# First two experts of a mixture-of-experts stage written out as straight code without scatter, weight turn and additions; counts loaded inside the first gather

## The reference

```
logits = h2 @ w_router + b_router;  top 4 of 32 experts per token, softmax over the four
for each expert e, over the tokens that chose it:
    hu   = xe @ w_up[e] + b_up[e]            # 1024 -> 2048
    gate = min(hu[:, :1024], 7);  lin = clip(hu[:, 1024:], -7, 7)
    y    = ((lin + 1) * gate * sigmoid(1.702 * gate)) @ w_down[e] + b_down[e]
    out[token] += weight(token, e) * y
x = x + gt_f * out;  y_out = rms_norm(x, g_final)
```

## Time and profile before

| | us |
|---|---|
| median of 3 runs | 1329.02 (1322.39 to 1330.13) |
| span of the profiled execution | 1322.8 |
| TensorE busy | 1189.2 (90%) |
| VectorE / ScalarE / GpSimd busy | 387.1 / 176.3 / 71.6 |
| data moved | 467.22 MB, mean 353 GB/s |

### The profile page before, as it was taken

One profiled execution on the slowest core, in us unless ns is written; L12 is line 12 of the kernel. 1 busy time (PEld: TensorE's weight loads), 2 busy tenths in 40 slices (PEclk: granted clock), 3 DMA queues, 4 the chain that ended last, 5 costly groups with the idle time before them and its releaser, 6 DMA issues.

```text
span 1322.8 us, 23572 instructions
## 1 busy us (share of the span) xinstructions
PE 1189.2 (90%) x8761; PEld 556.1 (42%) x8764; DVE 387.1 (29%) x857; ACT 176.3 (13%) x334; POOL 71.6 (5%) x180
## 2 busy tenths in 40 slices
PE   5999999898989999998999988999877989988996
PEld 4655447645534344443334432444222334333332
DVE  0173215737331221231222121132211221222225
ACT  3002231012101001010111100011110000110101
POOL 1010001323000000000000000000000000000001
PEclk9999999988989999998999998999988999989998
DMA  9934634784569999999999999999999999999992
GB/s 371 358 129 177 225 128 192 223 322 145 235 238 404 396 415 410 422 421 423 421 422 422 422 422 422 422 387 423 423 422 422 422 421 423 420 422 422 423 421 89
DMA packets 80911, 467.22 MB, mean 353 GB/s; under 512 B 8714, under 2 KB 26958, under 8 KB 28778
## 3 DMA queue, kind: packets, MB, share of 16 engines
q1 hardware_dynamic: 78202, 461.75, 85.8%
q10 hardware_dynamic: 2288, 4.37, 1.1%
q0 software_dynamic: 384, 0.59, 0.2%
HBM read 459.66 MB, written 6.42 MB: 352 GB/s over the span
## 4 chain that ended last, share of the span: by engine, by line
PE 65%; DMA 20%; SPq 8%; DVE 3%; issue 3%; POOL 0%; ACT 0%; POOLq 0%; DVEq 0%
PE psum L998 18%; DMA mem<-in_w_up 18%; PE psum L1036 12%; PE psum L1046 8%; SPq L417 7%; PE psum L650 6%; PE psum L965 4%; PE psum L631 3%; PE psum L837 2%; DMA mem<-in_mod_chunks 2%; PE psum L654 2%; PE psum L506 1%; PE psum L758 1%; PE psum L1054 1%; PE psum L1002 1%
## 5 line engine op out<-in xcount | busy, mean ns | idle before, releaser
L998 PE MATMUL psum<-mem 128*32 128x512 f32 (+2 forms) x2432 | 404.3, 626 | 83.8 <-DMA mem<-in_w_up 61.4
L998 PEld LDWEIGHTS psum<-mem 128*32 128x32 f32 (+2 forms) x2432 | 122.2, 122 | 357.5 <-issue 215.8
L1036 PE MATMUL psum<-mem 128*32 128x512 f32 (+3 forms) x1024 | 213.0, 598 | 0.0
L2066 DVE TENSOR_SCALAR mem<-psum 128x256 f32<-128x256 f32 (+3 forms) x32 | 19.2, 601 | 554.8 <-PE psum L1002 554.8
L1046 PE MATMUL psum<-mem 128*128 128x512 f32 (+1 forms) x384 | 152.2, 607 | 2.0 <-issue 1.5
L2087 DVE TENSOR_TENSOR mem<-mem,psum 128x1024 f32<-128x1024 f32 (+1 forms) x96 | 100.3, 1045 | 97.7 <-PE psum L1046 97.7
L1036 PEld LDWEIGHTS psum<-mem 128*32 128x32 f32 (+3 forms) x1024 | 79.6, 128 | 106.2 <-issue 100.0
L965 PEld LDWEIGHTS psum<-mem 128*128 128x128 bf16 x2304 | 77.5, 99 | 20.4 <-issue 20.1
L650 PE MATMUL psum<-mem 128*128 128x512 f32 x192 | 84.2, 595 | 0.0
L965 PE MATMUL psum<-mem 128*128 128x64 bf16 (+1 forms) x2304 | 81.3, 197 | 0.0
L1392 ACT ACTIVATE mem<-mem 128x256 f32<-128x256 f32 (+3 forms) x32 | 17.9, 559 | 465.7 <-DVE mem L2066 465.7
(11 more groups left out here) (275 smaller groups left out, 820.0 us busy)
## 6 DMA issues: line engine op xcount, KB each, us to landing
mem<-in_w_up SPq DMA_DIRECT2D x256, 1024.0 KB, 22.9
mem<-in_w_down SPq DMA_DIRECT2D x128, 1024.0 KB, 17.9
mem<-in_mod_chunks SPq DMA_DIRECT2D x12, 2048.0 KB, 12.2
mem<-in_in_chunks SPq DMA_DIRECT2D x8, 2048.0 KB, 9.8
mem<-in_out_chunks SPq DMA_DIRECT2D x2, 2048.0 KB, 10.0
mem<-in_x_prompt ACTq DMA_DIRECT2D x2, 1024.0 KB, 6.4
mem<-in_state_ret SPq DMA_DIRECT2D x4, 512.0 KB, 8.6
mem<-in_state_mlstm_c SPq DMA_DIRECT2D x4, 512.0 KB, 7.8
```

The source lines that it names most:

```text
L998: last = pe.matmul(out, xg[:, c, cols], moving, start=(c == 0), stop=False)
L1036: last[c] = pe.matmul(psum[slots * q:slots * q + slots, 6 + u, :], turned, piece_slot(home + c, 2, D)[:, piece % 2, 512 * u:512 * u + 512] ...
```

## The change

- The passes of experts 0 and 1 on TensorE are straight code (`expert_without_scatter`): no scatter, no waits on `added` and `y_copied`; pass 0 also has no turn of weights. Pass 1 turns the weights of expert 0 and runs `down(0)`. The loop starts at `FIRST = 2`, and the semaphore counts are shifted accordingly.
- VectorE does no `add_scattered` in passes 0 and 1; ScalarE copies no `G` in pass 0; GpSimd does not clear `G` and `yd`.
- TensorE loads the three first counts before `part2` of the first gather, not after the gather. VectorE computes the counts ahead of the last three `leave_rest` steps.

```diff
@@ gather_first
                 for part in range(3):
+                    if part == 2:
+                        pe.wait_ge(S("counts_ready"), 1)
+                        counted = [count_at(i) for i in range(1, 4)]
                     for t in range(NT):
...
+                return counted
@@ expert (TensorE)
-                gather(ig + 1, count_next, it + 1)
-
-                pe.wait_ge(S("G_ready"), it + 1)
-                pe.wait_ge(S("y_copied"), it + 1)
+                gather(ig + 1, count_next, it)
+
+                pe.wait_ge(S("G_ready"), it - 1)
+                pe.wait_ge(S("y_copied"), it - 1)
...
-                pe.wait_ge(S("added"), 3 * it + 1 + CLEARED)
+                pe.wait_ge(S("added"), 3 * (it - FIRST) + 1 + CLEARED)
...
+            def expert_without_scatter(it, count, count_before, count_next):
+
+                by_size(pe, count, lambda slots: up(it, it, slots))
+                gather(it + 1, count_next, it)
+                pe.wait_ge(S("xg_ready"), it + 2)
+                by_size(pe, count, lambda slots: turn_activations(it, slots))
+                pe.wait_ge(S("gate_ready"), it + 1)
+                pe.wait_ge(S("lin_clipped"), it + 1)
+                if it == 0:
+                    return
+                turn_weights(it, 2)
+                by_size(pe, count_before, lambda slots: down(it - 1, slots, False))
+                pe.wait_ge(S("G_ready"), it)
...
-            gather_first()
-            pe.wait_ge(S("counts_ready"), 1)
...
-            with pe.Fori(0, NE) as e:
+            first, second, third = gather_first()
+            expert_without_scatter(0, first, None, second)
+            expert_without_scatter(1, second, first, third)
+            with pe.Fori(FIRST, NE) as e:
@@ ScalarE
-            copy_gathered(0, None)
             act.wait_ge(S("counts_ready"), 1)
...
-            count = count_at(1)
-            take_up(0, 0, count, count_at(2))
-            copy_weights(0)
+            count, second, third = count_at(1), count_at(2), count_at(3)
+            copy_gathered(0, None)
+            take_up(0, 0, count, second)
             by_size(act, count, lambda slots: copy_turned(0, slots, False))
-            act.nop().then_inc(S("y_copied"), 1)
-            with act.Fori(1, NE) as e:
+            expert(0, 1, 1, second, third)
+            with act.Fori(FIRST, NE) as e:
@@ GpSimd
-            pool.memset(G, 0.0)
...
-            pool.memset(yd, 0.0).then_inc(S("yd_zero"), 1)
@@ VectorE
             one_hot(0, 0, 0)
-            leave_rest(2, 0)
-            leave_rest(1, 1)
-            leave_rest(2, 1)
             dve.memset(counts[:, 0:1], 0.0)
...
             dve.tensor_copy(counts_i, counts).then_inc(S("counts_ready"), 1)
+            leave_rest(2, 0)
+            leave_rest(1, 1)
+            leave_rest(2, 1)
...
-            weights(0, 0, count)
             by_size(dve, count, lambda slots: swiglu(0, slots))
-            add_scattered(0)
-            with dve.Fori(1, NE) as e:
+            expert(0, 1, 1, (0, 0), count_at(2), count)
+            with dve.Fori(FIRST, NE) as e:
```

More of the change, by code:

```diff
@@ L968, in products @@
                     last.then_inc(S("gathered"), 1)
-                if turned is not None:
+                if not isinstance(turned, int) or turned > 0:
                     pe.wait_ge(S("actT_ready"), turned)
@@ L1070, in expert @@
                 by_size(pe, count, lambda slots: turn_activations(it, slots))
-                pe.wait_ge(S("added"), 3 * it + 1 + CLEARED)
+                pe.wait_ge(S("added"), 3 * (it - FIRST) + 1 + CLEARED)
                 turn_weights(it, 2)
                 scatter(it, 2)
[L1074 to L1082, removed]
+                by_size(pe, count_before, lambda slots: down(it - 1, slots, False))
+                pe.wait_ge(S("G_ready"), it)
+                pe.wait_ge(S("added"), 3 * (it - FIRST) + 3 + CLEARED)
+            def expert_without_scatter(it, count, count_before, count_next):
[8 more added lines that the diff above has]
+                turn_weights(it, 2)
+                by_size(pe, count_before, lambda slots: down(it - 1, slots, False))
+                pe.wait_ge(S("G_ready"), it)
             def last_expert(its, count):
                 turn_weights(its, 1)
-                pe.wait_ge(S("y_copied"), its + 1)
+                pe.wait_ge(S("y_copied"), its - 1)
                 by_size(pe, count, lambda slots: down(its - 1, slots, True))
-                pe.wait_ge(S("G_ready"), its + 1)
+                pe.wait_ge(S("G_ready"), its - 1)
                 for u in range(2):
@@ L1118, in _ @@
                 for r in range(1, ROUNDS):
-                    gather(r * (NE + 1), None, r * NE + 1)
+                    gather(r * (NE + 1), None, r * NE)
                     expert(r, 0, r * NE, None, count_at(NE) if r == 1 else None, None)
@@ L1428, in last_expert @@
             def last_expert(its):
-                act.wait_ge(S("Pg_turned"), its + 1)
+                act.wait_ge(S("Pg_turned"), its)
                 act.copy(G_last, psum[:, 1, 0:NTOK]).then_inc(S("G_ready"), 1)
@@ L2078, in expert, with add_scattered @@
                 by_size(dve, count, lambda slots: swiglu(it, slots))
-                add_scattered(it)
-            def add_scattered(it):
+                if isinstance(it, int) and it < FIRST:
+                    dve.wait_ge(S("Pg_turned"), it)
+                    return
+                add_scattered(it - FIRST)
+            def add_scattered(n):
                 for t in range(NT):
-                    dve.wait_ge(S("scattered"), 3 * it + t + 1)
+                    dve.wait_ge(S("scattered"), 3 * n + t + 1)
                     v = acc[:, t, :] if t < 2 else acc[:, 2, 0:512]
```

26 lines of the change are left out of this document (11 added, 15 removed).

## The result

The changed kernel takes 1339.76 us in the median of ten runs (1334.96 to 1346.2), the kernel before 1329.58 us in ten runs (1322.39 to 1334.05). The medians are 10.2 us apart; the recorded ratio is 1.0087 with a 95% interval of 1.0066 to 1.0109: slower, where 10 us faster was forecast, and outside the range. The profiled execution has a span of 1335.8 us (time 1337.61), 13.0 us above the span of before.

A forecast was written before the change was run, and what follows sets the result against it. The weight stream's start and holes were taken as the bound. The stream would start 8.9 us earlier and close holes, capped by TensorE's lead of 10.0 us: 1329.0 - 10 = 1319 us, range 1310 to 1327.

The forecast's parts named there:

- What bounds the kernel: From 378 us on, the end is set by the weight stream's start plus its holes; the stream runs at 422 GB/s.
- Counts in the first gather: Around the first gather: 1.0 us gained before the first `up`, a 0.6 us gap for loads, 0.4 us earlier overall.
- Pass 0: Between gather(1) and `up(1)`: scatters and loop end vanish, branches cost 0.9 us, `up(1)` starts 8.1 us earlier, bounds 6.1 to 9.4.
- What straight code costs: TensorE in pass 1 and the loop's first pass: three cold jumps, 3.9 us, leaving a lead of 10.0 us at expert 3.
- the 1.53 us gap: TensorE's gap at 365.58 in the kernel before, its first run behind a skipped variant, taken as price of a cold jump.
- Clock: TensorE in `up(1)`: short idle stretches keep full clock, so it takes 7.4 us where it took 9.8.
- Sum: Whole kernel: stream early by 9.5 + 2.3 us, capped by TensorE's lead of 10.0 us, so the end moves 10 us.
- the clock of 0.50: Sign at `up(1)`: the forecast is wrong if its clock is 0.50; 1.00 was expected.
- the hole near 450: Sign in the weight stream: a hole of at most 2.3 us expected there; the forecast is wrong if it grows.
- Rival 1: After `up(1)` and `up(2)`: gaps of 2 us or more, or a clock drop; gain only 3 to 7 us; chance 0.20.
- Rival 4: Every loop pass: the loop no longer stays in TensorE's instruction memory and refetches; 58 us slower, 1377 us; chance 0.03.

The follow-up runs named there:

- hold_stream: The changed kernel with SyncE holding all loads behind the up pieces of expert 1 until down(0) has left its first piece; 1347.05 us in one run.
- peel_last: The kernel before with TensorE's pass of expert 31 as straight code behind a loop over 0 to 30; ratio to before 1.0087 (1.0056 to 1.0117).
- fixed_sizes: The changed kernel with TensorE's two straight passes cut to the one size variant these inputs take; ratio to before 1.0009 (0.9982 to 1.0037).
- guarded_loop: The kernel before's single loop from expert 0, with the change's omissions under branches on the expert's number; ratio to before 0.9987 (0.9964 to 1.001).
- before_late_counts: The kernel before with two of the three count loads of TensorE's loop head moved behind up; ratio to before 0.9974 (0.9953 to 0.9995).
- fixed_hold_loop: fixed_sizes with SyncE sending the up pieces of expert 2, then nothing until gather(3) has ended; 1346.72 us in one run.
- after_warm: The changed kernel with eight filler products behind gather(1), where the scatter of zeros stood before; 1347.27 us in one run.

## Why the prediction was wrong

- **What bounds the kernel** was right: the start of the stream and its holes. The holes account for 12.8 of 13.0 us. But the start by itself decides nothing: hold_stream lets the stream rest some 26 us and reaches `up(3)` and the end as the change does.
- **Counts in the first gather**: 0.6 us paid, 0.59 measured; 0.4 us gained, 0.45 measured. Right in size; the credit belonged to the loop's head. (The 0.59 us for all three loads speak against the 1.8 us that the forecast names as another price; its 0.2 us lost does not follow either, since half hidden they give 0.1 us gained.)
- **Pass 0**: `up(1)` at 367.3 forecast, 365.91 measured; branches cost nearly nothing there. SyncE asked again at 367.62, forecast 368.6.
- **What straight code costs** is the step that failed. "I count three cold jumps at the 1.53 us gap less the usual 0.24 between products, 1.3 us each: 3.9 us, bounds 0 and 8." Measured: gaps of 5.19, 1.93, 4.52, 6.12 and 2.28 us, 20.0 in all, of which up to 0.9 at the second is the wait for a copy. The kind of cost was right, and so were the ten more instruction packets before 450 us and none after them; count and price were not. The row was not short because the DMA engines were idle, their share was 0.82. It was short because its packet came 1.2 us before the gather ended, so that products covered a part of the 2.7 us from packet to restart. Behind `up(1)` and `up(2)` of the change the packets came 0.9 to 1.6 us after the end of the work, two at each place. And not only jumps pay: the 2.28 us lie between two products of one gather.
- **Clock**: wrong. I took full clock because the idle stretches were short; it fell to 0.50, and `up(1)` took 8.77 us, not 7.0. Price 1.7 us. And the term named only `up(1)`: behind the gaps the same low clock stretched gather(2) from 2.28 to 3.78 us, `down(0)` from 13.9 to 16.2 and gather(3) from 4.30 to 3.81 + 3.79, 7.1 us more.
- **Sum**: `up(3)` was to come 9.6 us earlier relative to the first `up`, 13.5 without cold jumps; it came 14.4 later. The 27.9 us between are what the gaps less the copy, 19.1, and the low clock, 8.8, come to; that it closes to the tenth is chance, since `up(1)` came 1.0 us earlier than forecast. Of the signs named, two came true: the clock of 0.50, and the hole near 450 grew, to 9.0 us at 432 to 442.5. Rival 1 had the mechanism, cold code and clock, and its place, but stopped at a gain of 3 us because it priced the gaps at 2 us. Rival 4 had the sign, but its mechanism is refuted: no instruction packet from 460 to 1300 us, and 422 GB/s late.

The page "Runtime: NRT & Kernel Launch" of the Trainium skill, section "Instruction fetch mechanics", says that a taken branch out of the current pages forces a fetch, and that crossing into the next page is mostly hidden. The first agrees with the gaps behind `up(1)` and `up(2)` and the packets in them. For the second, two gaps lie inside a gather, with no branch: 2.28 us here and 4.49 us in peel_last, with a packet at 425.8 and at 1292.1 us. If they are such crossings, which the packets suggest and do not prove, they were not hidden; those at 392.0 and 406.1 us, behind long products of `down(0)`, were.

Left open: why TensorE waits for the third packet of the loop's first pass behind `up(2)` in fixed_sizes (11.03 us) and inside the gather in the change (6.12 + 2.28), how much of each gap is the load and how much the place of the code in the fetched blocks, and what TensorE does in the 2.3 to 2.9 us behind a packet. All gaps are of one profiled execution each.

## What to carry to other kernels

Straight code in place of the first passes of a large loop is new code twice: once itself, and once when the loop begins. Here that was ten instruction packets and some 19 us of gaps, and 9 us more because the clock fell behind them. Special cases can stand in the loop under branches: guarded_loop leaves out the same work with no packet more, and was not slower; alone it was not clearly faster either. Before a gap is used as a price, ask what covered a part of it where it was read. And where TensorE must wait anyway, products that nobody reads can hold its clock: `up(1)` took 7.07 us for 8.77 or 9.75, though in the change that won nothing on the whole.

## What the runs showed of the hardware

- The same first-time code, under the weight stream and with idle DMA engines: gaps of 5.19 and 2.67 us, 4.52 (half of it loaded) and 1.87, 11.03 and 6.04.
- From the last instruction packet to the next product it was 2.3 to 2.9 us in nine gaps: 362.9 to 365.58 before, 383.0 to 385.80, 388.8 to 391.58 and 425.8 to 428.09 in the change, 369.9 to 372.57 in before_late_counts, 1286.3 to 1289.01 and 1292.1 to 1294.51 in peel_last, 415.5 to 418.26 in fixed_sizes, and with idle DMA engines 411.7 to 414.68 in fixed_hold_loop. In the two longest gaps of the change it was 3.7 and 4.5 us, behind `up(1)` of hold_stream 4.1.
- A loop whose passes repeat 30 times showed no instruction packet from 460 to 1300 us, jumps over skipped variants included; the pass of expert 2 took 34 us as the loop's first and 21.8 us when two passes had gone before it.
- The granted clock fell to 0.50 at 366.4 us while `up(1)` was already running, after TensorE had been busy for only 1.00 us of the stretch from 363.3 to 366.0 us; in after_warm, with fillers in that place, it stayed at 1.00 from 374 to 383 us. At 0.50 a gather's product took 112 ns for 60.
